# Attention inner step on one core: the turns of a tile's probabilities ahead of the values of the tile before it

## What is computed

```python
def attend(args):
    q_blk, b = args
    q_chunk = (b * Q_BLOCK + jnp.arange(Q_BLOCK)) // CHUNK
    mask = key_chunk[None, :] <= q_chunk[:, None]
    s = jnp.einsum('bqhd,bkhd->bhqk', q_blk, k).astype(jnp.float32) * scale
    s = jnp.where(mask[None, None], s, neg)
    prob = jax.nn.softmax(s, axis=-1).astype(v.dtype)
    return jnp.einsum('bhqk,bkhe->bqhe', prob, v)
```

## Time and profile before

| what | value |
| --- | --- |
| median of 3 runs | 1261.47 us (1260.75 to 1261.95) |
| the profiled execution's own time | 1259.99 us |
| its span in the profile | 1258.2 us |
| PE busy | 1235.3 us, 98% of the span |
| DVE / POOL / ACT busy | 727.2 / 508.8 / 484.1 us |
| mean granted TensorE clock | 0.998 |

### The profile page before, as it was taken

The page is one execution under the profiler, slowest core; times in us unless marked ns, Lnnn a source line. Parts: engine busy times, 40 slices in busy tenths (PEclk is TensorE's granted clock), DMA queues, the critical chain, the costliest instruction groups (busy, mean ns, idle before and its releaser), DMA issues.

```text
span 1258.2 us, 16749 instructions
## 1 busy us (share of the span) xinstructions
PE 1235.3 (98%) x6008; PEld 1040.3 (83%) x6008; DVE 727.2 (58%) x1186; ACT 484.1 (38%) x879; POOL 508.8 (40%) x514
## 2 busy tenths in 40 slices
PE   9999999989999999999999999999999999999997
PEld 8888888868898888888888888888888888888886
DVE  5544444486665427855444555444489999955433
ACT  6622222245664214633333333333354334524422
POOL 2533344440000002555433555334399889810011
PEclk9999999999999999999999999999999999999999
DMA  9511111010021500233423423323454555420002
GB/s 340 164 34 51 34 35 34 1 43 1 0 67 68 151 1 1 76 111 99 126 81 88 126 93 116 116 77 100 169 182 160 193 167 184 151 84 1 1 34 101
DMA packets 101932, 115.10 MB, mean 91 GB/s; under 512 B 4832, under 2 KB 67680, under 8 KB 101856
## 3 DMA queue, kind: packets, MB, share of 16 engines
q1 hardware_dynamic: 101424, 113.57, 27.8%
q10 hardware_dynamic: 432, 0.54, 0.1%
HBM read 90.49 MB, written 23.59 MB: 91 GB/s over the span
## 4 chain that ended last, share of the span: by engine, by line
PE 93%; DVE 3%; issue 2%; POOL 1%; ACT 1%; DMA 0%; POOLq 0%; DVEq 0%; SPq 0%; ACTq 0%
PE PS L1671 11%; PE PS L1670 11%; PE PS L1669 11%; PE PS L206 7%; PE PS L208 7%; PE PS L207 7%; PE PS L2003 5%; PE PS L2004 5%; PE PS L2005 5%; PE PS L996 3%; PE PS L1012 3%; PE PS L2358 2%; PE PS L2360 2%; PE PS L2359 2%; PE PS L790 2%
## 5 line engine op out<-in xcount | busy, mean ns | idle before, releaser
L206 PE MATMUL PS<-WF,HTH 128*128 128x512 f32 (+1 forms) x448 | 176.5, 394 | 3.0 <-DVE WF L184 1.5
L208 PE MATMUL PS<-WF,HTL 128*128 128x512 f32 (+1 forms) x448 | 173.4, 387 | 0.0
L207 PE MATMUL PS<-WF,HTH 128*128 128x512 f32 (+1 forms) x448 | 173.0, 386 | 0.0
L1390 DVE TENSOR_TENSOR X<-X,PS 128x512 f32<-128x512 f32 x172 | 110.2, 678 | 53.3 <-PE PS L208 35.2
L1669 PE MATMUL PS<-HTH,WF 128*128 128x512 f32 x336 | 130.7, 389 | 0.0
L1670 PE MATMUL PS<-HTL,WF 128*128 128x512 f32 x336 | 130.7, 389 | 0.0
L1671 PE MATMUL PS<-HTH,WF 128*128 128x512 f32 x336 | 130.7, 389 | 0.0
L1602 DVE TENSOR_TENSOR WF<-RAW,WF 128x512 fp32r<-128x512 f32 x63 | 70.9, 1127 | 77.5 <-ACT WF L1592 77.5
L206 PEld LDWEIGHTS PS<-WF,HTH 128*128 128x128 f32 x448 | 84.2, 188 | 19.1 <-DVE WF L184 1.9
L1669 PE MATMUL PS<-WF 128*128 128x512 f32 x252 | 98.0, 389 | 0.0
L1670 PE MATMUL PS<-WF 128*128 128x512 f32 x252 | 98.0, 389 | 0.0
(11 more groups left out here) (254 smaller groups left out, 2806.3 us busy)
## 6 DMA issues: line engine op xcount, KB each, us to landing
hid<-TMP SPq DMA_DIRECT2D x74, 256.0 KB, 2.3
TMP<-hid SPq DMA_DIRECT2D x25, 512.0 KB, 4.6
RAW<-in_w_ffn_gate SPq DMA_DIRECT2D x22, 512.0 KB, 4.2
RAW<-in_w_ffn_up SPq DMA_DIRECT2D x22, 512.0 KB, 5.4
RAW<-in_w_ffn_down SPq DMA_DIRECT2D x22, 512.0 KB, 4.2
X<-in_x SPq DMA_DIRECT2D x16, 512.0 KB, 6.6
RAW<-in_w_in SPq DMA_DIRECT2D x32, 256.0 KB, 3.8
TAB<-hid SPq DMA_DIRECT2D x9, 512.0 KB, 4.6
```

Of the source, the lines that this page charges most:

```text
L206: nc.tensor.matmul(dst, HTH[:, k, tok], w_h, start=(k == 0), stop=False)
L207: nc.tensor.matmul(dst, HTH[:, k, tok], w_l, start=False, stop=False)
L208: last = nc.tensor.matmul(dst, HTL[:, k, tok], w_h, start=False, stop=(k == K - 1))
L1390: nc.vector.tensor_tensor(x, x, src, ALU.add).then_inc(done, 1)
```

## The change

In each step of PE's loop over the tiles of a head, T(t) is issued ahead of V(t-1) instead of behind it. Everything else is the same, the waits inside `turn` and `values` too, and no other engine's program changes.

```diff
@@ -1023,9 +1023,9 @@
 
                     e.wait_ge(a_exp, h * T + T - 1)
                     early(t + 2 - T)
+                turn(t)
                 if t >= 1:
                     values(t - 1)
-                turn(t)
             e.wait_ge(a_exp, h * T + T)
             after(lambda: values(T - 1))
```

## The result

The changed kernel takes 1266.49 us as a median of 6 runs (1265.42 to 1266.78), against 1261.54 us for the kernel before (6 runs, 1260.13 to 1262.11). The ratio is 1.0040, with a 95% interval of 1.0028 to 1.0052: it is slower by 3.5 to 6.6 us. The forecast was 1265.8 us, in a range of 1263.0 to 1268.4.

A forecast was written before the change was run, and what follows sets the result against it. PE was taken to bound the kernel, busy 98% of the span, with no slack behind the heads. The terms 0.27 + 2.61 + 0.88 + 0.54 = 4.3 us on 1261.47 gave 1265.8 us, range 1263.0 to 1268.4.

The forecast's parts named there:

- (b): Who waits for the late copy(t): only T(7), 0.09 us in each of the first three heads, 0.27 us together.
- (c): End of the first three heads: V(6) ends later by T(7), delaying copy(7) and V(7) by 0.87 us each, 2.61 us.
- (d): Start of each head: V(0) no longer fits PE's wait for tile 1's division, 0.22 us each, 0.88 us.
- (e): End of the fourth head: T(6), T(7) and the chain to the first output product each get 0.18 us, together 0.54.
- (a): On ACT, copy(t) starts later, behind out_hi(t-1), which waits for V(t-1): 0.26 us in the loop, 0.18 in the fourth head.
- Rival C: The delay at the heads' ends is not passed on to the next head: 1.7 us left, 1263.2 us; chance 0.10.
- (f): T(t) needs its probabilities one V(t-1) sooner; 0.30 us are left at the narrowest place, tile 2, so nothing is lost.
- (g): Operand kinds change in another order on PE: exposed loads could cost 2.8 us at worst, taken as nothing.
- Rival D: More waits than counted, for probabilities or exposed loads: at worst 2.8 us more, 1268.6 us; chance 0.12.
- Rival B: Copy(t) runs beside V(t-1), so PE's waits for copies and of V(0) go: 3.06 us gained, 1258.4 us; chance 0.03.

The follow-up runs named there:

- the last experiment: Both kernels unchanged, profiled and timed once more: kernel before 1261.11 us, changed kernel 1265.53 us, ratio 1.0031.
- experiment 6: Changed kernel with the new PE order in steps 2 to 6 alone, steps 1 and 7 as before: 1262.26 us, ratio 1.0004 to the kernel before.
- experiment 4: Changed kernel with the new PE order in step 7 of each head alone: 1264.93 us, ratio 1.0021 to the kernel before.
- experiment 5: Changed kernel with step 1 alone put back, V(0) ahead of T(1): 1266.39 us, ratio 1.0035 to the kernel before.
- experiment 1: Changed kernel with copy(t) written ahead of out_hi(t-1) on ScalarE: 1259.02 us, ratio 0.9974 to the kernel before.
- the second: Kernel before with copy(t) written ahead of out_hi(t-1) on ScalarE, PE's order untouched: 1262.40 us, ratio 1.0001 to the kernel before.
- experiment 3: Changed kernel with the two query casts written ahead of out_hi(6) on ScalarE in step 7: 1263.08 us, ratio 1.0008 to the kernel before.

## Why the prediction was right

The sum was 4.30 us; the stretch of the heads grew by 4.42, and the medians by 4.95 with 3.5 to 6.6 as their interval. On the chip of the last experiment the medians differ by 3.61 us (1265.53 and 1261.92), 0.81 below 4.42 where the first pair was 0.53 above: the stretch is the size to hold the sum against. The terms, as the experiments separate them:

| term | predicted, us | measured, us | from |
| --- | --- | --- | --- |
| (b) T(6), T(7) wait in the first three heads | 0.27 | 0.61 | experiment 6, heads 0 to 2 |
| (c) V(7) at the end of the first three heads | 2.61 | 2.66 | experiment 4, heads 0 to 2 |
| (d) V(0) no longer in the wait for tile 1 | 0.88 | 0.64 | experiment 5 |
| (e) end of the fourth head | 0.54 | 0.53 | experiments 4 and 6, head 3 |
| sum | 4.30 | 4.44 | |

In experiment 6 it is V(6), not T(7), that waits for copy(6), as the order of step 7 is the old one. The measured terms add up to what the change as a whole cost (4.42), so the pieces hardly influence each other.

- (a), copy(t) held back by out_hi(t-1), is shown by experiment 1, which takes the holding away, and by the second, in which the same edit wins nothing without PE's new order. Its size was right: in experiment 6 copy(5) begins 17.80 us behind the first scores in head 0 (310.34 - 292.54) and began at 17.53 in the kernel before (308.16 - 290.63), 0.27 us later where I had 0.26; in the fourth head it is 0.18, as taken. In the profile after, T(7) of head 0 lies ready for 1.7 us before ACT has out_hi(6) to do.
- (b) was sized too small. I gave T(6) nothing and T(7) 0.09 us a head, and it is some 0.05 and 0.15, 0.20 for both: I compared the copy's end with the start of the first pass (309.32 with 309.35), but the load ahead of it starts earlier (309.12) and is exposed when it has to wait. T(6) shows it (load idle for 0.26 us, no wait of the matmul), and in experiment 1 the other side of it, V(7) shorter by 0.24 us.
- (c) was right, and it passed in full into the next head. The 0.96 us by which the two casts delayed copy(7) account, times three, for the 2.9 us of experiment 3. Rival C falls.
- (d) had the right mechanism, T(1) released by the division at the same time as before, and too high a size: two passes among others cost 0.16 us and not the 0.22 that I took from an average of fourteen. The two errors, 0.34 us too little in (b) and 0.24 too much in (d), nearly cancel: that the sum comes so near to 4.42 is in part luck.
- (f) and (g) are nothing in the changed kernel, as taken: no T but T(0) and T(1) waits for a division (T(6) of the fourth head begins at 400.14, behind copy(5), which ends at 399.99), and steps 2 to 5 lose nothing (experiment 6). It is the late copy that hides (f) at that T(6): in experiment 1, without it, the division is 0.28 us late. Rival D falls with experiment 6.
- Rival B, the values hide the copy, is wrong for this change, since copy(t) never began before V(t-1) ended. But it named what the change lacked: once ScalarE makes the copy first, the waits for the copies go, and the two edits together win 2.17 us where PE's alone had lost 4.42. That is the overlap which the Trainium skill (Perfetto Trace Analysis, Optimizing Tensor Performance, Matmuls) asks for, evacuation of one group beside the matmuls of the next, and the trace of experiment 1 agrees, with no wait ahead of V(7) in the first three heads. Rotating the groups over banks was not enough without the order of the evacuations.

## What to carry to other kernels

Before two groups are swapped on the busiest engine, look at the order in which the engine behind it takes their results: a copy that stands behind another group's copy inherits that group's end, however early its own data are ready. Swap both or neither. Where an order is to hide a wait, find first what the moved piece itself had been hidden in; here V(0) had been free.

## What was not expected

The granted TensorE clock falls for some microseconds ahead of the heads in 8 of the 11 profiles of this case, whichever kernel runs (a mean of 0.90 to 0.93 between 240 and 292 us, against 1.00 in the other three). Windows of the kernel before, first profile and second profile (stretch, length, busy by engine, clock, DMA share, GB/s):

```profile
260.00:270.00 10.00, 5.97 (x39) 4.70 (x40) 8.62 (x24) 3.26 (x7) 3.69 (x9) 1.00 0.01 2
270.00:280.00 10.00, 9.95 (x70) 8.76 (x69) 8.94 (x24) 5.50 (x10) 5.81 (x12) 1.00 0.00 0
```

```profile
260.00:270.00 10.00, 6.28 (x33) 5.36 (x34) 8.14 (x23) 3.39 (x8) 3.69 (x9) 0.77 0.01 2
270.00:280.00 10.00, 10.00 (x52) 8.97 (x52) 6.75 (x19) 3.33 (x6) 4.04 (x8) 0.72 0.00 0
```

With a mean of 0.77 and 0.72 the clock stood at its lower level (1.2 GHz) for about half of these 20 us, and the first scores come at 293.82 us instead of 290.63. It falls in the stretch in which PE is busy for only some 6 of 10 us, but PE was busy for as little there where the clock stayed up. In the changed kernel it was 0.80 and 0.86 there. Of that kernel's 2.32 us, 0.6 were there before the clock fell (the same matmul of line 606 begins at 257.44 us, and at 256.82 in the kernel before); the rest came behind that. Over all the profiles the first scores came between 290.63 and 293.82 us. For the two profiles of the kernel before, this is nearly all of their difference (3.19 of 3.3 us); for the runs without a profile it isn't shown. It is why a difference of two profiled executions has to be split by stretches before it is laid to a change. What decides in which executions the clock falls stays open.
